# Forget attention with the forget sums as a row of query and key, in place of a product that picks them

## The reference

```python
def fox_attention(q, k, v, log_f):
    scale = 1.0 / math.sqrt(d_)
    F = jnp.cumsum(log_f, axis=-1)
    ...
    s = jnp.einsum('bhqd,bhkd->bhqk', qi, k).astype(jnp.float32) * scale
    s = s + Fi[..., None] - F[:, :, None, :]
    s = jnp.where(mask, s, -jnp.inf)
    p = jax.nn.softmax(s, axis=-1)
    return jnp.einsum('bhqk,bhkd->bhqd', p.astype(v.dtype), v)
    ...
hn = rmsnorm(h, norm_mix_g[l]); proj = hn @ w_in[l]
log_f = jax.nn.log_sigmoid(ff + fox_f_bias[l])
h = h + jnp.concatenate([fox_out, rec], axis=-1) @ w_out[l]
```

## Time and profile before

| what | value |
| --- | --- |
| median of 3 runs | 900.51 us (900.48 to 901.94) |
| the profiled execution's own time | 901.04 us |
| its span in the profile | 899.3 us |
| TensorE / VectorE / ScalarE / POOL busy | 890.8 / 607.9 / 488.6 / 106.8 us |
| granted TensorE clock | 0.999 of full speed |
| HBM read | 157.81 MB, 177 GB/s over the span |

### The profile page before, as it was taken

The page is one execution under the profiler, slowest core; times in us unless marked ns, Lnnn a source line. Parts: engine busy times, 40 slices in busy tenths (PEclk is TensorE's granted clock), DMA queues, the critical chain, the costliest instruction groups (busy, mean ns, idle before and its releaser), DMA issues.

```text
span 899.3 us, 15856 instructions
## 1 busy us (share of the span) xinstructions
PE 890.8 (99%) x6305; PEld 821.5 (91%) x6305; DVE 607.9 (68%) x813; ACT 488.6 (54%) x726; POOL 106.8 (12%) x136
## 2 busy tenths in 40 slices
PE   9999999999999999999999999999999999999997
PEld 9988988888989999988899989999999899999886
DVE  5795875965646766544466538898686788888643
ACT  7766545635646555533373346664644666666432
POOL 6421132200000000000035070001000100000000
PEclk9999999999999999999999999999999999999999
DMA  9958632244533856565547554345556386676631
GB/s 293 304 172 285 213 127 94 57 179 141 198 119 102 261 187 189 196 201 201 195 140 235 199 188 142 123 134 169 181 173 191 110 234 187 188 195 202 209 141 47
DMA packets 135266, 159.63 MB, mean 177 GB/s; under 512 B 3951, under 2 KB 113773, under 8 KB 134957
## 3 DMA queue, kind: packets, MB, share of 16 engines
q1 hardware_dynamic: 133261, 151.79, 53.0%
q0 software_dynamic: 1344, 6.03, 1.9%
q10 hardware_dynamic: 608, 1.06, 0.3%
HBM read 157.81 MB, written 1.05 MB: 177 GB/s over the span
## 4 chain that ended last, share of the span: by engine, by line
PE 91%; DVE 3%; ACT 2%; DMA 1%; issue 1%; SPq 1%; POOL 0%; DVEq 0%; POOLq 0%; ACTq 0%
PE tb L698 16%; PE tb L700 16%; PE tb L699 16%; PE acc L698 11%; PE acc L699 11%; PE acc L700 11%; PE acc L992 1%; DMA raw<-in_w_in 1%; DVE wlo L1945 1%; PE tb L949 1%; DVE wlo L1869 1%; ACT whi L1330 0%; PE tb L1183 0%; PE acc L1213 0%; PE tb L1086 0%
## 5 line engine op out<-in xcount | busy, mean ns | idle before, releaser
L1869 DVE TENSOR_TENSOR wlo<-raw,whi 128x2048 fp32r<-128x2048 f32 x138 | 316.9, 2301 | 178.5 <-ACT whi L1330 177.8
L1330 ACT ACTIVATE whi<-raw 128x2048 fp32r<-128x2048 f32 x138 | 264.1, 1915 | 181.3 <-PE acc L700 119.0
L698 PE MATMUL tb<-xhi,whi 128*128 128x256 f32 x1192 | 331.8, 278 | 0.7 <-DVE wlo L1869 0.6
L700 PE MATMUL tb<-xhi,wlo 128*128 128x256 f32 x1192 | 329.3, 276 | 0.0
L699 PE MATMUL tb<-xlo,whi 128*128 128x256 f32 x1192 | 329.3, 276 | 0.0
L698 PEld LDWEIGHTS tb<-xhi,whi 128*128 128x128 f32 x1192 | 223.8, 188 | 1.5 <-issue 1.4
L699 PEld LDWEIGHTS tb<-xlo,whi 128*128 128x128 f32 x1192 | 223.9, 188 | 0.1
L700 PEld LDWEIGHTS tb<-xhi,wlo 128*128 128x128 f32 x1192 | 223.8, 188 | 0.0
L698 PE MATMUL acc<-whi,hid_hi 128*128 128x512 f32 x128 | 50.0, 390 | 0.0
L700 PE MATMUL acc<-whi,hid_lo 128*128 128x512 f32 x128 | 49.8, 389 | 0.0
L699 PE MATMUL acc<-wlo,hid_hi 128*128 128x512 f32 x128 | 49.8, 389 | 0.0
(11 more groups left out here) (408 smaller groups left out, 1528.7 us busy)
## 6 DMA issues: line engine op xcount, KB each, us to landing
raw<-in_w_in SPq DMA_DIRECT2D x37, 1024.0 KB, 5.2
raw<-in_w SPq DMA_DIRECT2D x32, 1024.0 KB, 5.3
raw<-in_w_up SPq DMA_DIRECT2D x44, 512.0 KB, 5.0
raw<-in_w_down SPq DMA_DIRECT2D x22, 512.0 KB, 4.1
raw<-in_w_xkv SPq DMA_DIRECT2D x8, 1024.0 KB, 6.0
raw<-in_w_out SPq DMA_DIRECT2D x8, 1024.0 KB, 5.2
raw<-in_w_mem_kv SPq DMA_DIRECT2D x4, 1024.0 KB, 5.1
raw<-in_w_xq SPq DMA_DIRECT2D x4, 1024.0 KB, 5.0
```

The source lines that it names most:

```text
L698: pe.matmul(o, a_hi, b_hi, start=start, stop=False)
L700: return pe.matmul(o, a_lo, b_hi, start=False, stop=stop)
L1330: act.activation(whi[:, n % RING, :m], raw[:, n % RING, :m], ACT.Copy).then_inc(hi_ready, 1)
L1869: dve.tensor_tensor(low(n), raw[:, n % RING, :m], whi[:, n % RING, :m].bitcast(F32), ALU.subtract).then_inc(lo_ready, 1)
```

## The change

Query and key get a place for each of the eight heads with 128 partitions by 256 tokens: `fq` (new room) and `fk` (a view of `h`). Head i stands in the partitions of its half (even heads 0 to 63, odd 64 to 127). The other half is zero but for one partition (64 or 0): ones in `fq`, -F of head i in `fk`. A product over all 128 partitions then gives the score with -F added. `pick` and the four `negF` operations go (`negF` itself stays for the first products of the program, on zeros).

POOL clears `fq` and `fk`, scales 128x1024 at a time (`scale_heads`), writes the ones and copies the eight rows of -F by DMA. ScalarE empties by halves of the partitions. Since `fk` covers `x`, SyncE waits for the last scores after the first slab of `w_out` and loads `x` again, and VectorE waits for that before the residual.

```diff
-        pick = sb("pick", [P, FOX_H], F32R)
+        sb("gap_k", [P, FOX_H])
...
-                fqT = sb("fqT", [P, 4, T], at=r1)
-                fkT = sb("fkT", [P, 4, T], at=r1)
+                fq = sb("fq", [P, FOX_H, T], at=r1)
...
+        fk = h[:, :, :].rearrange("p t (a c) -> p (t a) c", c=T)
+
+        def heads(t, c, n, r):
+
+            return t[64 * r:64 * r + 64, 2 * c + r:2 * (c + n):2, :]
...
                 else:
                     load(n)
+                if n == first["wo"]:
+                    sp.wait_ge(fox["scores"], 8)
+                    for q in range(4):
+                        load_x(q)
...
-            pool.memset(causal[:, :], 0.0)
-            pk = small[:, 0:FOX_H]
-            link(pool.tensor_tensor(pk, ident[:, 0:FOX_H], ident[:, 32:32 + FOX_H], ALU.add))
-            link(pool.tensor_tensor(pk, pk, ident[:, 64:64 + FOX_H], ALU.add))
-            link(pool.tensor_tensor(pick[:, :], pk, ident[:, 96:96 + FOX_H], ALU.add))
+            link(pool.memset(causal[:, :], 0.0))
...
             pool.dma_start(xn[:, :, :], w["mem"].rearrange("(t p) c -> p t c", p=P)).then_inc(mem_in, 16)
+            pool.memset(fq[:, :, :], 0.0)
             rms("x")
+            pool.memset(fk, 0.0).then_inc(fx["empty"], 1)
             rms("mem")
...
+            def scale_heads(n, t, c):
+
+                pool.wait_ge(act_emptied, act_evacs[n])
+                s = t[:, 2 * c:2 * c + 4, :]
+                link(pool.tensor_tensor(s, s, fs[:, 1, 0:T].rearrange("p (a t) -> p a t", a=1).broadcast_to([P, 4, T]), ALU.mult))
+                pool.sem_inc(x_scaled, 1)
...
             for j in range(2):
-                scale_x(first["fq"] + j, fqT[:, 2 * j:2 * j + 2, :])
+                scale_heads(first["fq"] + j, fq, 2 * j)
+            link(pool.memset(fq[64:65, 0:FOX_H:2, :], 1.0))
+            link(pool.memset(fq[0:1, 1:FOX_H:2, :], 1.0))
+            pool.sem_inc(fx["one"], 1)
             for j in range(2):
-                scale_x(first["fk"] + j, fkT[:, 2 * j:2 * j + 2, :])
+                scale_heads(first["fk"] + j, fk, 2 * j)
+            pool.wait_ge(fx["F"], 1)
+            for i in range(FOX_H):
+                r = 64 - 64 * (i % 2)
+                pool.dma_start(fk[r:r + 1, i, :].rearrange("a (c t) -> a c t", c=2), am[i:i + 1, 10:12, :]).then_inc(fx["row"], 16)
             pool.wait_ge(ml["lo"], 4)
...
-                    pe.wait_ge(fx["F"], 1)
+                    pe.wait_ge(fx["one"], 1)
+                    pe.wait_ge(fx["row"], 16 * FOX_H)
...
-                p0, c = (i % 2) * 64, i // 2
                 for o, s, t in ((tb[:, 2, 0:P], P, 0), (tb[:, 2, P:384], T, 1)):
-
-                    pe.matmul(o, pick[p0:p0 + 64, i:i + 1].broadcast_to([64, P]), negF[p0:p0 + 64, 0:s], start=True, stop=False)
-                    last = pe.matmul(o, fqT[p0:p0 + 64, c, t * P:t * P + P], fkT[p0:p0 + 64, c, 0:s], start=False, stop=True)
+                    last = pe.matmul(o, fq[:, i, t * P:t * P + P], fk[:, i, 0:s], start=True, stop=True)
...
+            def empty_heads(n, t, c, scale=1.0):
+
+                act.wait_ge(slab_done, n + 1)
+                for r in range(2):
+                    s = tb[64 * r:64 * r + 64, X_BANK[n], :].rearrange("p (c t) -> p c t", c=2)
+                    last = act.activation(heads(t, c, 2, r), s, ACT.Copy, scale=scale)
+                last.then_inc(act_emptied, 1)
+
             n = first["fq"]
-            empty_pair(n, fqT[:, 0, :], fqT[:, 1, :], 0.125)
+            act.wait_ge(fx["empty"], 1)
+            act.wait_ge(slab_done, n + 1)
+            for r in range(2):
+                for c, s in enumerate((tb[64 * r:64 * r + 64, X_BANK[n], 0:T], second_bank(n)[64 * r:64 * r + 64])):
+                    last = act.activation(fq[64 * r:64 * r + 64, 2 * c + r, :], s, ACT.Copy, scale=0.125)
+            last.then_inc(act_emptied, 1)
...
-            empty(n, fqT[:, 2:4, :], ACT.Copy, tb[:, X_BANK[n], :], scale=0.125).then_inc(act_emptied, 1)
+            empty_heads(n, fq, 2, 0.125)
...
-                empty(n, fkT[:, 2 * j:2 * j + 2, :], ACT.Copy, tb[:, X_BANK[n], :]).then_inc(act_emptied, 1)
+                empty_heads(n, fk, 2 * j)
...
+                if name == "h1":
+                    for q in range(4):
+                        dve.wait_ge(x_in[q], 32)
                 add(0)
...
-            link(dve.tensor_tensor_scan(sf, zf, am[0:8, 8:10, :].rearrange("p a c -> p (a c)"), 0.0, ALU.add, ALU.add))
-            dve.wait_ge(consts_ready, 2)
-            for r in (64, 0):
-                last = dve.tensor_copy(negF[r:r + 8, :], sf)
-            link(last)
-            for r in (32, 96):
-                last = dve.tensor_tensor(negF[r:r + 8, :], sf, negF[0:8, :].bitcast(F32), ALU.subtract)
-            last.then_inc(fx["F"], 1)
+            dve.tensor_tensor_scan(sf, zf, am[0:8, 8:10, :].rearrange("p a c -> p (a c)"), 0.0, ALU.add, ALU.add).then_inc(fx["F"], 1)
```

More of the change, by code:

```diff
@@ L268, in two_blocks @@
         hg = sems("hg", "ln sf sq qs d e z prod merged out sq2 ss rs rec rd gsig gg kk")
-        fx = sems("fx", "z l F")
+        fx = sems("fx", "z l F row empty one")
         fox = sems("fox", "scores read max exp p pt ptc pv pvhi pvlo")
```

## The result

The changed kernel takes 903.49 us (median of 17 runs, 902.34 to 905.81) against 900.81 (17 runs) for the kernel before: ratio 1.0031, 95% interval 1.0025 to 1.0038. The forecast was 902.1, range 898.4 to 904.2. So the time lies inside the range and on the forecast's side, but 1.4 us above it (0.3 of that is the kernel before, which measured 900.81 and not the 900.5 that the forecast started from), and past the bound of 0.2% behind which I had put only 0.32 of the chance.

The account below looks back on a forecast made before the run. TensorE, busy 890.8 of 899.3 us, was taken to bound the kernel. Stalls of 2.8 us less 1.2 us gained in the loop gave +1.6 on 900.5, so 902.1 us, with a range of 898.4 to 904.2.

Parts of the forecast that it names:

- the bound of 0.2%: Smallest change a measurement tells from none (1.8 us); chance 0.32 slower than that (above 902.3), 0.15 faster.
- The doubled scaling: Input projections: POOL's 128x1024 scalings take 2.6 us instead of 1.30 and block VectorE throughout; 2.8 us lost in all.
- Slab 7: Input projections: VectorE's low half ends at 48.3 instead of 46.94, delaying TensorE by 1.3 us.
- two of VectorE's small operations slip ahead: Before slab 7: two VectorE operations go before POOL's scaling, which then runs from 42.2 to 44.8.
- Slab 10: Input projections: low half waits behind POOL's second key scaling; start at 66.6, bringing the loss to 2.8 us in all.
- only slab 7 is hit: Rival: slab 10's low half gets in between the two key scalings; +0.1 us, 900.6; chance 0.17.
- The loop: Eight steps of forget attention: 1.2 us gained of a possible 3.4 from the removed picking products.
- The chain is last: Loop steps: slab's end over ScalarE and VectorE to POOL's last multiplication outlasts TensorE's shortened work by 0.6 us.
- The load of x and the eight row transfers: Reload of x before the residual, and POOL's row transfers of some 6.2 us from 67.12: no cost to time.
- The clearings: POOL clears two 128x2048 tiles, about 1.9 us each, in its 5.67 us of idleness before 24.68: no cost.
- the rival of 904.0: Rival: POOL's two 0.95 us memsets take turns with VectorE's low halves, moving everything behind by 1.9 us; chance 0.13.
- Within 0.2%: Outcome that the whole kernel's time stays between 898.7 and 902.3 us; chance 0.53.

Follow-up runs that it names:

- e1_narrow_scaling: The changed kernel with POOL's four scalings over 128x512 instead of 128x1024, the other heads left unscaled; 900.38 us, ratio 0.9996 to the kernel before.
- e5_load_later: The changed kernel with POOL's clearing of the query tile put ahead of its load of the first memory; 902.64 us, ratio 1.0022 to the kernel before.
- e2_busy_wait: The changed kernel with nine unread matmuls of 128 columns put before slab 7 of the input projections; 903.46 us.
- e7_level_early: The changed kernel with level differences (VectorE) ahead of each step's weight work and level exponentials (ScalarE) ahead of attention's; 903.38 us, ratio 1.0027.
- e3_no_pick: The kernel before without the picking products, so the forget term is left out of the scores; 900.04 us, ratio 0.9991.
- e4_scale_late: The changed kernel with POOL's scalings, memsets of ones and row transfers moved behind VectorE's low half of slab 12; 900.27 us, ratio 0.9997.
- e11_before_mask_early: The kernel before with the levels' differences and attention's masks early on VectorE; 900.33 us, ratio 0.9999.
- e10_mask_early: The changed kernel with scalings, ones and row transfers late, first memory's load later, level differences and attention's masks early; 896.41 us, ratio 0.9948 to the kernel before.

## Why the prediction came out as it did

**The doubled scaling: right, and the whole story ahead of the loop.** Where nothing held them up, POOL's operations took 2.4 to 2.65 us (2.6 taken), VectorE was held up to their end, and TensorE waited for the low half. e1_narrow_scaling takes the width away and the loss goes. This is how the Trainium skill (SBUF — State Buffer, "SBUF: two separate sides") describes the pair, an exclusive lock for the whole instruction; the trace agrees in both directions, 1.95 and (e5_load_later) 2.39 us on VectorE's side, 4.07 on POOL's.

**Slab 7: too small.** The term "two of VectorE's small operations slip ahead", with +1.3 us, failed. The first of them did not slip ahead: it was caught (1.95 us), and the other two came behind the scaling. The delay is 1.87 us counted from slab 0. The start of the scaling was right within 0.2 us (0.69 later than in before, counted from slab 0; 0.9 forecast); what was wrong is how much of VectorE's work was left behind it.

**Slab 10: absent here.** The +1.5 us for it stand in e2_busy_wait by the way given, so the mechanism is a true one. In the changed kernel the order of arrival was another, since TensorE ran late behind slab 7: here the rival "only slab 7 is hit" was right. Its time of 900.6 was not, for it had 1.3 us for slab 7 and nothing for the clock.

**The clock: missing.** No row of before has a wait of TensorE above 1.3 us, and I priced a wait at its own length. This one cost 2.49 and then 1.5 more. In sum 3.14 ahead of the loop stand against a forecast of 2.8. That this is close is luck: the +1.5 forecast for slab 10 did not come, and 1.5 us that I had not thought of stood in its place. Without the loss of clock and without the stall the same sum would have been 3.14 - 1.5 = 1.6.

**The loop: right in kind, 0.6 too high in size, and too simple.** I took 1.2 of 3.4 us; it gave 0.63. The level starts relative to the first scores were earlier by 0.15, 0.41, 0.35, 0.87, 0.62, 0.97, 1.37 and 0.64 us (forecast 0.35, 0.4, 0.55, 0.95, 0.8, 0.95, 1.4, 1.2), and the products of levels 2 to 7 start within 0.15 us of POOL's end, so the chain over POOL carried for these. The first and the last are off: the transposes of step 1 wait 0.77 us for the normalised rows, and the last level 0.22 us for a merge, 0.98 us behind POOL. "The chain is last" was true, but not "the only one": e7_level_early took it away and gained 0.37; only with attention's chain gone as well did the loop give 4.6 (4.1 against the kernel before with the same moves). And the possible gain was not 3.4: the transposes and the HGRN products on either side of the scores got shorter by 0.1 us each in most steps. Nor is it all due to the picking products. Their removal alone makes a head's scores 0.23 us shorter (e3_no_pick); the other 0.20, and the 0.1 on either side, came only with the products over 128 partitions.

**What was costed at nothing.** The load of x and the eight row transfers show no wait behind the loop (713.9 us in both). The eight row transfers took POOL 3.9 us, not 6.2, from 67.00 on. The clearings fit where they were put. One of them did hold up VectorE:

```profile
19.37 1.16 DVE L2003 TENSOR_SCALAR small<-small 128x4 f32<-128x4 f32 x1
...
18.70 1.81 POOL L614 MEMSET h<- 128x2048 f32 x1
```

Four elements took 1.16 us, to just behind the clearing's end at 20.51; VectorE was idle after it anyway. The low halves were not touched: the one at 56.14 (2.29 us) ran across POOL's memset of ones at 57.05 (0.94) at its usual length. POOL's first memset of ones did meet VectorE, but its copy: it lasted 1.29 us instead of 0.94, and nothing waited for it. So the rival of 904.0, whose time came near, was wrong in its mechanism, as the rule of the Trainium skill quoted beside it said: the low halves have two inputs in SBUF, the two operations that met a memset have one.

**The chances.** The bound of 0.2% lay at 902.3, and the forecast 0.2 below it. The result passed it by 1.2, its repeat (903.22) by 0.9. "Within 0.2%" had the most of the chance with a forecast that stood next to its edge; 0.6 us too much in the loop and 0.3 too little ahead of it were enough to cross it, with 0.3 more from the kernel before.

## What to carry to other kernels

When a change takes work off the engine that bounds the kernel, look for all chains that hang on the same event, not the latest alone: here the first removed chain gave 0.4 us and the second 3.6. Work that a chain carries behind a wait, though it needs nothing of what is waited for (here mask and difference behind the low half), is the first thing to move. And an operation on POOL should not be doubled in width next to a VectorE queue without slack: it costs VectorE its whole length, at a place that some tenths decide.

## What was unexpected of the hardware

TensorE's clock fell to half behind a wait of 2.13 (e7_level_early) to 2.49 us, for matmuls that began 0.5 to 0.8 us after work had started again, and was full again some 3 us later; the changed kernel, its repeat, e5_load_later and e7_level_early all show 0.72 in the window of 47 to 53 us. It did not fall where nine matmuls filled the first microsecond of that wait and 1.46 us were left (e2_busy_wait), nor behind the 1.56 us at slab 10 in that kernel, nor behind 0.83 us (e4_scale_late). A wait of 2.5 us thus had a price of 4.

A scan and a copy on VectorE were held up as well as operations on 8 partitions or one column: what POOL's scaling costs VectorE does not depend on how small VectorE's operation is (128x1 took 2.30 us).

A float32 score product over 64 partitions was dearer than one over 128. A head's four matmuls took 0.85 us over 64 partitions (e3_no_pick) and 0.65 over 128 (after). The transposes ahead of them took 0.42 against 0.33 us and the HGRN products behind them 1.93 against 1.82 (e11_before_mask_early and e10_mask_early). In e11_before_mask_early itself the last transposes, which have no scores behind them, take 0.33 as well. So the cost appears where products over 64 and over 128 partitions follow each other; that the change of partitions is the cause was not tested by itself.
